# The down matrices of a mixture of experts loaded in two units of adjacent rows, with the middle rows turned at a stride

## The chip, the cores and the metric

The kernel runs on one core of a Trainium2 chip. The metric is the device time of one execution in microseconds (us); lower is better.

## What is computed

Two layers of a first block (three attention mixers side by side, a layer norm, a mixture of experts with a gated side path, a second norm), then two layers of a second block, all on 256 tokens of width 1024, in float32. The change touches the experts of the first block and little else. What counts there is this (16 experts, each 1024 x 512 for gate and up, 512 x 1024 for down; every token picks two experts):

```
scores = sigmoid(h @ router_w)            # choose 1 of 4 groups, then 2 of its 4 experts
gate = one_hot(idx) * wts                 # weights of the two chosen
out = 0
for e in range(16):
    hid = silu(h @ w_gate[e]) * (h @ w_up[e])
    out = out + gate[..., e:e + 1] * (hid @ w_down[e])
h = layer_norm(alpha * h + out + side_path)
```

## The kernel before

**Weights.** All weights are streamed from HBM in units of 1 MB, 128 partitions x 2048 values, in one fixed list (`weight_plan`; for the experts `add_experts`). SyncE issues one DMA per unit (L379) into one of up to six raw buffers as soon as VectorE has read the unit that was there before. ScalarE rounds the unit to a high part (`split_scalar`, L387, two halves of 1024), VectorE subtracts to get the low part (`split_vector`, L392, two halves), and TensorE multiplies with both. There are three split buffers, so ScalarE's split of a unit waits until TensorE has finished with the unit three places earlier. `Feed` makes both engines split two units ahead: when an engine's program reaches the use of unit u, it first splits unit u + 2.

**An expert.** Each expert e has six units: gate 0 and 1, up 0 and 1, and then down 0 and 1 of expert e - 1. At most 64 tokens go to an expert in the fast path; `pick` gathers the tokens of four experts at once. High and low parts of the 64 tokens lie side by side as 128 columns, so that one pass with the high and one with the low part of the weights is a whole product. TensorE does, in iteration e:

- gate product of e, 16 matmuls of 512 columns (`up`, L1448 and L1451)
- `add_to_tokens(e - 2, 1)`: four matmuls (L1494) that put the second 512 columns of the result of e - 2 back into the token rows (in PSUM banks 4 to 7)
- `turn_hidden(e - 1)`: 8 float32 matmuls (16 passes in the trace, L1473) that turn the gate and up rows, 128 columns each, so that the hidden values lie along the partitions
- up product of e, 16 matmuls; after every fourth expert also `pick` (L1434, L1442)
- down products of e - 1, for each half of the output columns 8 matmuls
- `add_to_tokens(e - 1, 0)`: four matmuls for the first 512 columns

The order is written out by hand in the same way for ScalarE and VectorE; every engine works through its own list in order and waits on semaphores. After the turn ScalarE takes silu (L1572), VectorE multiplies (L1709), ScalarE makes the high part (L602), VectorE the low part (L605). After a half of the down product ScalarE scales it and writes the high part (L1583), VectorE the low part (L1718) into the single tile pair `expert_rows_hi` / `expert_rows_lo`, 512 wide; so ScalarE's second write waits for the first half's adds ("add e 0"). GpSimd makes the matrix that puts rows back to tokens (L1750) after the last adds of the expert before.

**Layout of a down unit.** Unit `half` holds the 512 columns of that half of all 512 rows: partition p holds rows p, 128 + p, 256 + p and 384 + p, in four runs of 2 KB. The turned hidden rows stand in the same order.

**Other tiles.** `junk` (128 x 1024) takes the unread output of squares (L655, L675), the sigmoids of the side path, and some start tables. `arena` is one tile from which views are cut by `mem(start, n)`.

Of the kernel before, what the change touches and what calls it, by code (L numbers as in the profile page):

```python
# [8 lines left out]
I32 = mybir.dt.int32  # L9
# [245 lines left out]
def build(nc, a, out):  # L255
    with ExitStack() as ctx:
# [15 lines left out]
        junk = sb("junk", [P, D])  # L272
# [8 lines left out]
        y_e = (sb("expert_rows_hi", [P, 512], F32R), sb("expert_rows_lo", [P, 512], F32R))  # L281
# [339 lines left out]

        gained = mem(6144, NT * D).rearrange("p (t d) -> p t d", t=NT)
# [29 lines left out]
        def norm_squares(act, label, t):  # L652
            act.wait_ge(*sig.now("junk_act"))
            act.wait_ge(*sig.at("norm_dve", f"{label} mean{t}"))
            act.activation(junk[:, :], h[:, t, :], ACT.Square, bias=stat[t][:, 1:2],  # L655
# [16 lines left out]
        def squares(act, src, total, *label):  # L672

            act.wait_ge(*sig.now("junk_act"))
            act.activation(junk[:, 0:src.shape[1]], src, ACT.Square, accum_out=total).then_inc(*sig.mark("junk_act", *label))  # L675
# [36 lines left out]
        pos_i = junk[:, 0:2 * S].bitcast(I32).rearrange("p (a s) -> p a s", a=2)  # L712
        posk = junk[:, S:2 * S]
        lam_in = junk[:, 512:1024].rearrange("p (j l n) -> p j l n", l=DEPTH, j=4)
# [343 lines left out]
        def scalar_block1(act, feed, tables, l):  # L1058
# [81 lines left out]
            for t in range(NT):  # L1140
# [3 lines left out]
                for hd in range(4):  # L1144
                    squares(act, orow1[:, t, hd, :], so1[:, 4 * t + hd:4 * t + hd + 1], n_("diff squares"))
# [226 lines left out]
        sg_of = lambda i: junk[:, 512 * (i % 2):512 * (i % 2) + 512]  # L1372
# [3 lines left out]
        def tensor_experts(pe, l):  # L1376
# [111 lines left out]
            def add_to_tokens(e_, half):  # L1488
                if half == 0:
                    pe.wait_ge(*sig.at("moe_pool", n_(f"rows {e_}")))  # L1490
                pe.wait_ge(*sig.at("dve_took", n_(f"down {e_} {half}")))
                for t in range(NT):
                    for part in range(2):
                        last = pe.matmul(PS[:, 4 + 2 * t + half, :], from_slot[:, t * P:(t + 1) * P], y_e[part][:, :],  # L1494
                                         start=e_ == 0 and part == 0, stop=e_ == N_EXP - 1 and part == 1)
                    if t == 0 and half == 1 and e_ == N_EXP - 1:
                        last.then_inc(*sig.mark("ps", n_("ln2") + " t0"))
                last.then_inc(*sig.mark("ps", n_(f"add {e_} {half}")))
# [27 lines left out]
        def scalar_experts(act, feed, l):  # L1526
# [50 lines left out]
            def down(e_, half):  # L1577
                name = n_(f"down {e_} {half}")
                feed(name)
                act.wait_ge(*sig.at("ps", n_(f"add {e_} 0") if half else name))  # L1580
                if half == 0:
                    act.wait_ge(*sig.at("dve_took", n_(f"pick gate {e_ // GROUP}")))
                act.activation(y_e[0][:, :], PS[:, banks.of(name), :], ACT.Copy,  # L1583
                               scale=gate_of(e_ // GROUP)[:, e_ % GROUP:e_ % GROUP + 1]).then_inc(*sig.mark("moe_act", name))

            pick(0)
            for e_ in range(N_EXP + 1):
# [8 lines left out]
                if e_ > 0:  # L1596
                    down(e_ - 1, 0)
                    down(e_ - 1, 1)
# [64 lines left out]
        def vector_experts(dve, feed, l):  # L1663
# [50 lines left out]
            def down(e_, half):  # L1714
                name = n_(f"down {e_} {half}")
                feed(name)
# [824 lines left out]
```

## Time and profile before

| | us |
|---|---|
| median of 3 runs | 1946.6 |
| lowest, highest | 1943.07, 1947.17 |
| the profiled execution | 1943.74 |
| its span (first to last instruction) | 1942.5 |
| TensorE busy in it | 1801.3 (93%) |
| VectorE busy | 1362.5 (70%) |
| ScalarE busy | 1134.9 (58%) |
| GpSimd busy | 180.4 (9%) |

The rows below come from this one execution. Its own time stands 1.2 us above the span. Busy time of TensorE is modelled at its ends, so a busy engine need not be at its peak. Times in rows are microseconds from the start of the span; durations in the chain of waits are the time by which a piece moved the chain forward.

### The profile page before, as it was taken

What the parts mean: (1) busy time and instruction counts of PE and PEld (TensorE: products, weight loads), DVE (VectorE), ACT (ScalarE), POOL (GpSimd) and SP (SyncE); (2) the same over time, 40 slices, a digit from 0 to 9 for tenths busy, and PEclk for the clock granted to TensorE, in tenths of its full rate; (3) what the DMA queues carried; (4) which work ended last, traced back from release to release, by engine and by line L of the source; (5) the groups of instructions that cost most, each with busy time, mean ns of one, the idle gap of its engine ahead of it and who ended that gap; (6) DMA issues with size and microseconds to landing.
All of it is one profiled execution on the core that took longest, in us unless ns stands there. A gap on an engine that the chain in (4) does not pass through costs nothing.

```text
span 1942.5 us, 27994 instructions
## 1 busy us (share of the span) xinstructions
PE 1801.3 (93%) x11460; PEld 1565.2 (81%) x11460; DVE 1362.5 (70%) x1605; ACT 1134.9 (58%) x1574; POOL 180.4 (9%) x152
## 2 busy tenths in 40 slices
PE   6989998998799898989989999999999999999998
PEld 5867776776598687777768889988898989988987
DVE  6776999899737689989975675575556666566555
ACT  4565678788537468888864545444444644444443
POOL 1000412301000032321010000000000000000000
PEclk9889999999889999999989999999999999999999
DMA  8334599998552459999865545646555545555552
GB/s 250 111 114 173 223 346 346 339 331 331 185 150 88 140 200 382 326 334 358 324 239 170 159 131 174 197 150 217 174 195 171 179 131 159 181 181 184 193 188 87
DMA packets 209444, 413.19 MB, mean 213 GB/s; under 512 B 16384, under 2 KB 130816, under 8 KB 192928
## 3 DMA queue, kind: packets, MB, share of 16 engines
q1 hardware_dynamic: 208224, 409.76, 61.2%
q8 instruction: 95, 1.56, 0.3%
q10 hardware_dynamic: 1088, 1.57, 0.3%
q14 instruction: 37, 0.30, 0.0%
HBM read 409.47 MB, written 1.84 MB: 212 GB/s over the span
## 4 chain that ended last, share of the span: by engine, by line
PE 69%; DVE 22%; ACT 5%; issue 2%; DMA 1%; POOL 0%; SPq 0%; DVEq 0%; ACTq 0%
DVE weights_lo L392 14%; PE PS L407 10%; PE PS L411 10%; PE PS L408 10%; PE PS L415 7%; PE PS L418 6%; PE PS L419 6%; PE PS L1448 4%; PE PS L1451 4%; PE PS L1494 3%; PE PS L1473 3%; ACT weights_hi L387 2%; PE PS L1434 1%; DVE expert_rows_lo L1718 1%; PE PS L434 1%
## 5 line engine op out<-in xcount | busy, mean ns | idle before, releaser
L392 DVE TENSOR_TENSOR weights_lo<-weights_raw,weights_hi 128x1024 fp32r<-128x1024 f32 x564 | 661.0, 1218 | 210.0 <-ACT weights_hi L387 209.2
L387 ACT ACTIVATE weights_hi<-weights_raw 128x1024 fp32r<-128x1024 f32 x564 | 560.7, 1045 | 125.3 <-PE PS L419 76.3
L407 PE MATMUL PS<-hT_hi,weights_hi 128*128 128x256 f32 (+1 forms) x1488 | 427.4, 287 | 18.0 <-ACT weights_hi L387 11.5
L411 PE MATMUL PS<-hT_hi,weights_lo 128*128 128x256 f32 (+1 forms) x1488 | 424.5, 285 | 1.2 <-DVE weights_lo L392 1.2
L408 PE MATMUL PS<-hT_lo,weights_hi 128*128 128x256 f32 (+1 forms) x1488 | 424.4, 285 | 0.0
L407 PEld LDWEIGHTS PS<-hT_hi,weights_hi 128*128 128x128 f32 (+1 forms) x1488 | 285.1, 192 | 25.2 <-issue 19.7
L411 PEld LDWEIGHTS PS<-hT_hi,weights_lo 128*128 128x128 f32 (+1 forms) x1488 | 285.0, 192 | 2.4 <-DVE weights_lo L392 1.9
L408 PEld LDWEIGHTS PS<-hT_lo,weights_hi 128*128 128x128 f32 (+1 forms) x1488 | 285.2, 192 | 1.8
L392 DVE TENSOR_TENSOR weights_lo<-arena,weights_hi 128x1024 fp32r<-128x1024 f32 x128 | 150.9, 1220 | 16.4 <-ACT weights_hi L387 15.5
L415 PE MATMUL PS<-weights_hi,opa_hi 128*128 128x512 f32 x384 | 153.5, 400 | 3.0 <-DVE opa_lo L605 2.8
L418 PE MATMUL PS<-weights_lo,opa_hi 128*128 128x512 f32 x384 | 152.5, 397 | 0.0
L419 PE MATMUL PS<-weights_hi,opa_lo 128*128 128x512 f32 x384 | 152.2, 396 | 0.0
L387 ACT ACTIVATE weights_hi<-arena 128x1024 fp32r<-128x1024 f32 x128 | 128.1, 1051 | 0.0
L415 PE MATMUL PS<-weights_hi,hT_hi 128*128 128x256 f32 (+2 forms) x384 | 120.6, 314 | 2.1 <-DVE hT_lo L605 1.8
L670 POOL TENSOR_TENSOR small<-small,const 128x1 f32<-128x1 f32 (+2 forms) x26 | 20.9, 806 | 1085.3 <-DVE small L641 842.6
L418 PE MATMUL PS<-weights_lo,hT_hi 128*128 128x256 f32 (+2 forms) x384 | 119.0, 310 | 0.1
L419 PE MATMUL PS<-weights_hi,hT_lo 128*128 128x256 f32 (+2 forms) x384 | 118.9, 310 | 0.0
L1750 POOL TENSOR_SCALAR opb_lo<-arena,const 128x256 fp32r<-128x256 f32 x32 | 72.8, 2275 | 440.4 <-PE PS L1494 440.4
L1448 PE MATMUL PS<-weights_hi,hT_hi 128*128 128x512 f32 x256 | 103.7, 405 | 0.3
L1451 PE MATMUL PS<-weights_lo,hT_hi 128*128 128x512 f32 x256 | 101.4, 396 | 0.3 <-DVE weights_lo L392 0.3
L1451 PE MATMUL PS<-weights_lo,hT_lo 128*128 128x512 f32 x256 | 101.3, 396 | 0.4 <-DVE weights_lo L392 0.4
L1448 PE MATMUL PS<-weights_hi,hT_lo 128*128 128x512 f32 x256 | 101.2, 395 | 0.0
(322 smaller groups left out, 3192.1 us busy)
## 6 DMA issues: line engine op xcount, KB each, us to landing
weights_raw<-in_w_in SPq DMA_DIRECT2D x80, 1024.0 KB, 5.7
weights_raw<-in_w_ff SPq DMA_DIRECT2D x64, 1024.0 KB, 5.3
weights_raw<-in_w_up SPq DMA_DIRECT2D x34, 1024.0 KB, 7.2
weights_raw<-in_w_down SPq DMA_DIRECT2D x34, 1024.0 KB, 7.3
weights_raw<-in_w_gate SPq DMA_DIRECT2D x30, 1024.0 KB, 7.3
arena<-in_w_down SPq DMA_DIRECT2D x30, 1024.0 KB, 6.8
arena<-in_w_gate SPq DMA_DIRECT2D x18, 1024.0 KB, 7.0
params<-in_w_gate SPq DMA_DIRECT2D x16, 1024.0 KB, 6.6
```

Source lines behind the costliest of these rows:

```text
L387: act.activation(u.flat[0][:, c:e], u.x[:, c:e], ACT.Copy).then_inc(*sig.mark("w_hi", u.u, i))
L392: dve.tensor_tensor(u.flat[1][:, c:e], u.x[:, c:e], u.flat[0][:, c:e].bitcast(F32), ALU.subtract).then_inc(*sig.mark("w_lo", u.u, i))
L407: pe.matmul(o, w[0], x[0], start=start, stop=False)
L408: pe.matmul(o, w[0], x[1], start=False, stop=False)
L411: return pe.matmul(o, w[1], x[0], start=False, stop=stop)
L415: pe.matmul(o, x[0], w[0], start=start, stop=False)
L418: pe.matmul(o, x[0], w[1], start=False, stop=False)
L419: return pe.matmul(o, x[1], w[0], start=False, stop=stop)
L1448: pe.matmul(o, x, w[0], start=start, stop=False)
L1451: return pe.matmul(o, x, w[1], start=False, stop=stop)
L1473: last = pe.matmul(PS[:, b, (4 * j + c) * SLOTS:(4 * j + c + 1) * SLOTS], gate_up[e_ % 2][:, j, c * P:(c + 1) * P], fold, start=True, stop ...
L1750: pool.tensor_scalar(from_slot, slot_b[:, e_, :], col(COL_PART), None, ALU.is_equal).then_inc(*sig.mark("moe_pool", n_(f"rows {e_}")))
```

## The change

1. `add_experts`: a down matrix is cut by rows. Partition p holds rows 4p to 4p + 3; unit i holds rows 4p + 2i and 4p + 2i + 1, all 1024 columns, one run of 8 KB for a partition.
2. `turn_hidden`: to match, the columns of a block c are those with index 4f + c, taken at a stride of four values (16 bytes).
3. Down product: both units feed both output halves, each half in its own PSUM bank; for the last expert the first half is finished before the second is begun.
4. `expert_rows` has a place for each half. The adds of both halves of expert e - 2 stand together, after the gate product of e and after the turn of e - 1. ScalarE and VectorE split the next two units, and then take the two halves.
5. `junk` is gone; what was written there goes to parts of `arena`.

```diff
-        for half in range(2 if e > 0 else 0):
-            w = a["w_down"][l, e - 1][:, 512 * half:512 * half + 512]
-            plan.append((f"down {e - 1} {half} {l}", w.rearrange("(k p) n -> p k n", p=P), 4, 512))
+        for i in range(2 if e > 0 else 0):
+            w = a["w_down"][l, e - 1].rearrange("(p k) n -> p k n", p=P)
+            plan.append((f"down {e - 1} {i} {l}", w[:, 2 * i:2 * i + 2, :], 2, D))
...
-        junk = sb("junk", [P, D])
...
-        y_e = (sb("expert_rows_hi", [P, 512], F32R), sb("expert_rows_lo", [P, 512], F32R))
+        y_e = (sb("expert_rows_hi", [P, 2, 512], F32R), sb("expert_rows_lo", [P, 2, 512], F32R))
...
-        posf = mem(8192, 512).rearrange("p (a s) -> p a s", a=2)
+        posf = mem(4608, 512).rearrange("p (a s) -> p a s", a=2)
...
-        sg_of = lambda i: junk[:, 512 * (i % 2):512 * (i % 2) + 512]
+        sg_of = lambda i: mem(9216 + 512 * (i % 2), 512)
...
-                                         gate_up[e_ % 2][:, j, c * P:(c + 1) * P], fold, start=True, stop=True)
+                                         gate_up[e_ % 2][:, j, :].rearrange("p (f c) -> p c f", c=4)[:, c, :], fold, start=True,
+                                         stop=True)
...
-            def down(e_, half):
-                name = n_(f"down {e_} {half}")
-                u = use(pe, name)
-                b = banks.take(pe, name, "dve_took", among=4)
-                if half == 0:
-                    pe.wait_ge(*sig.at("moe_dve", n_(f"hidden {e_}")))
-                for k in range(4):
-                    last = two_pass(PS[:, b, :], hid_e[e_ % 2][:, k, :, :].rearrange("p c s -> p (c s)"), u,
-                                    at_k(u.pair, k, 0, 512), k == 0, k == 3, k == 0)
-                last.then_inc(*sig.mark("ps", name))
...
+            def down(e_):
+
+                us = [units[place[n_(f"down {e_} {i}")]] for i in range(2)]
+                b = [banks.take(pe, n_(f"down {e_} half {half}"), "dve_took", among=4) for half in range(2)]
+                parts = [(i, half) for i in range(2) for half in range(2)]
+                if e_ == N_EXP - 1:
+                    parts = [(i, half) for half in range(2) for i in range(2)]
+                pe.wait_ge(*sig.at("moe_dve", n_(f"hidden {e_}")))
+                for i, half in parts:
+                    fresh = half == 0
+                    if fresh:
+                        use(pe, us[i].name)
+                    for k in range(2):
+                        last = two_pass(PS[:, b[half], :], hid_e[e_ % 2][:, 2 * i + k, :, :].rearrange("p c s -> p (c s)"), us[i],
+                                        at_k(us[i].pair, k, 512 * half, 512 * half + 512), i == k == 0, i == k == 1,
+                                        fresh and k == 0)
+                    if half == 1:
+                        last.then_inc(*sig.mark("ps", us[i].name))
+                        if i == 1:
+                            sig.also("ps", n_(f"down {e_} half 1"))
+                    elif i == 1:
+                        last.then_inc(*sig.mark("ps", n_(f"down {e_} half 0")))
...
             for e_ in range(N_EXP + 1):
                 if e_ < N_EXP:
                     up(e_, "gate")
-                if e_ > 1:
-                    add_to_tokens(e_ - 2, 1)
                 if e_ > 0:
                     turn_hidden(e_ - 1)
+                if e_ > 1:
+                    add_to_tokens(e_ - 2)
                 if e_ < N_EXP:
                     up(e_, "up")
                     if e_ % GROUP == GROUP - 1 and e_ + 1 < N_EXP:
                         pick(e_ // GROUP + 1)
                 if e_ > 0:
-                    down(e_ - 1, 0)
-                    down(e_ - 1, 1)
-                    add_to_tokens(e_ - 1, 0)
-            add_to_tokens(N_EXP - 1, 1)
+                    down(e_ - 1)
+            add_to_tokens(N_EXP - 1)
...
-            def down(e_, half):
-                name = n_(f"down {e_} {half}")
-                feed(name)
-                act.wait_ge(*sig.at("ps", n_(f"add {e_} 0") if half else name))
-                if half == 0:
-                    act.wait_ge(*sig.at("dve_took", n_(f"pick gate {e_ // GROUP}")))
-                act.activation(y_e[0][:, :], PS[:, banks.of(name), :], ACT.Copy,
-                               scale=gate_of(e_ // GROUP)[:, e_ % GROUP:e_ % GROUP + 1]).then_inc(*sig.mark("moe_act", name))
+            def down(e_):
+                feed(n_(f"down {e_} 0"), n_(f"down {e_} 1"))
+                act.wait_ge(*sig.at("dve_took", n_(f"pick gate {e_ // GROUP}")))
+                for half in range(2):
+                    name = n_(f"down {e_} half {half}")
+                    act.wait_ge(*sig.at("ps", name))
+                    if e_ > 0:
+                        act.wait_ge(*sig.at("ps", n_(f"add {e_ - 1} {half}")))
+                    act.activation(y_e[0][:, half, :], PS[:, banks.of(name), :], ACT.Copy,
+                                   scale=gate_of(e_ // GROUP)[:, e_ % GROUP:e_ % GROUP + 1]).then_inc(*sig.mark("moe_act", name))
...
```

VectorE's `down` changes in the same way as ScalarE's (feed both units, then both halves), and `add_to_tokens` now loops over both halves and waits, before each, for VectorE's low part of that half.

## Rows read from the trace of the kernel before

**Rows 1.** The page's chain that ended last, by engine and by line.
```profile
PE 69%; DVE 22%; ACT 5%; issue 2%; DMA 1%; POOL 0%; SPq 0%; DVEq 0%; ACTq 0%
DVE weights_lo L392 14%; PE PS L407 10%; PE PS L411 10%; PE PS L408 10%; PE PS L415 7%; PE PS L418 6%; PE PS L419 6%; PE PS L1448 4%; PE PS L1451 4%; PE PS L1494 3%; PE PS L1473 3%; ACT weights_hi L387 2%; PE PS L1434 1%; DVE expert_rows_lo L1718 1%; PE PS L434 1%
```
**Rows 2.** Stretches, two experts: length, busy PE, PEld, DVE, ACT, POOL; clock, DMA, GB/s.
```profile
307.20:324.76 17.56, 15.58 (x74) 12.06 (x74) 15.95 (x17) 14.38 (x19) 2.29 (x1) 1.00 0.96 344
324.76:342.34 17.58, 15.61 (x74) 12.06 (x74) 16.00 (x17) 14.43 (x19) 2.32 (x1) 1.00 0.98 351
```
**Rows 3.** Chain of waits through one expert: start us, us, piece.
```profile
324.76 1.75 PE PS L1473 x16
...
328.81 6.90 DVE weights_lo L392 x6
335.71 0.67 DVE expert_rows_lo L1718
...
336.51 1.16 PE PS L1494 x4
337.68 0.24 PE PS L1448
...
341.41 0.92 PE PS L1494 x4
```
**Rows 4.** VectorE's timeline in two experts: start, us, instruction [idle before <- releaser].
```profile
326.94 0.42 DVE L1709 TENSOR_TENSOR arena<-arena,PS 128x256 f32<-128x256 f32 x1 [0.48 <-ACT arena L1572]
...
327.85 0.42 DVE L605 TENSOR_TENSOR opb_lo<-arena,opb_lo 128x256 fp32r<-128x256 f32 x1 [0.48 <-ACT opb_lo L602]
...
328.81 2.36 DVE L392 TENSOR_TENSOR weights_lo<-arena,weights_hi 128x1024 fp32r<-128x1024 f32 x2 [0.53 <-ACT weights_hi L387]
...
357.23 0.75 DVE L1718 SCALAR_TENSOR_TENSOR expert_rows_lo<-PS,small,expert_rows_hi 128x512 fp32r<-128x512 f32 x1 [0.35 <-ACT expert_rows_hi L1583]
...
358.18 2.36 DVE L392 TENSOR_TENSOR weights_lo<-arena,weights_hi 128x1024 fp32r<-128x1024 f32 x2 [0.20 <-ACT weights_hi L387]
```
**Rows 5.** L1709 from 232.1 to 492.9: idle before it, us and times.
```profile
  ACT arena L1572: 6.1, 13
```
**Rows 6.** L1473, the weight loads of all turns: ns min/median/max.
```profile
L1473 PEld LDWEIGHTS PS<-const,arena x512: 187/192/333, 231.9 to 1007.1; 128*128 128x128 f32 x171
```
**Rows 7.** L602 and L605: reads of h (strided) and of dense tiles, ns min/median/max.
```profile
L602 ACT ACTIVATE opa_hi<-h x4: 2319/2327/2332, 190.9 to 691.2; 128x1024 fp32r<-128x1024 f32 x4
L602 ACT ACTIVATE hT_hi<-arena x2: 1040/1048/1056, 6.4 to 7.3; 128x1024 fp32r<-128x1024 f32 x2
...
L605 DVE TENSOR_TENSOR opa_lo<-h,opa_hi x4: 2140/2182/2228, 198.2 to 698.5; 128x1024 fp32r<-128x1024 f32 x4
L605 DVE TENSOR_TENSOR hT_lo<-arena,hT_hi x2: 1219/1222/1226, 7.5 to 8.6; 128x1024 fp32r<-128x1024 f32 x2
```
**Rows 8.** SyncE's waits (us, times, longest); issues and landings of two units.
```profile
SPq L379 <- DVE weights_lo L392: 1555.5, 355, 21.0
...
313.63 0.38 SPq L379 DMA_DIRECT2D arena<-in_w_down  x1
...
318.17 0.34 SPq L379 DMA_DIRECT2D weights_raw<-in_w_gate  x1
...
arena<-in_w_down SPq DMA_DIRECT2D x1, 1024.0 KB, 7.8
...
weights_raw<-in_w_gate SPq DMA_DIRECT2D x1, 1024.0 KB, 8.4
```
**Rows 9.** Tail of layer 0: timeline, then one stretch as in rows 2.
```profile
499.65 2.35 DVE L392 TENSOR_TENSOR weights_lo<-arena,weights_hi 128x1024 fp32r<-128x1024 f32 x2
...
505.65 0.50 PE L1494 MATMUL PS<-expert_rows_hi,opb_lo 128*128 128x512 f32 x1 [1.66 <-DVE expert_rows_lo L1718]
...
510.50 0.77 PE L1448 MATMUL PS<-weights_hi,opb_lo 128*128 128x512 f32 x1 [1.93 <-DVE opb_lo L605]
...
519.61 1.22 DVE L628 SCALAR_TENSOR_TENSOR h<-h,PS 128x1024 f32<-128x1024 f32 x1 [0.82 <-PE PS L1494]
...
511.00:514.50 3.50, 3.50 (x11) 2.71 (x10) 2.24 (x2) 1.20 (x2) 0.00 (x0) 0.62 0.04 8
```

More of the change, by code:

```diff
@@ L620, in turned_lo @@
                 lo_part(dve, hT[1][sl], one_bank(banks.of(name), 4), hT[0][sl]).then_inc(*sig.mark("dve_took", name))
+        unread, unread2 = mem(8192, D), mem(6144, 512)
         gained = mem(6144, NT * D).rearrange("p (t d) -> p t d", t=NT)
@@ L670, in rstd, with squares @@
             return pool.tensor_tensor(dst, var, col(COL_NHALF).to_broadcast([P, var.shape[1]]), ALU.pow)
-        def squares(act, src, total, *label):
+        def squares(act, src, total, *label, dst=None):
             act.wait_ge(*sig.now("junk_act"))
-            act.activation(junk[:, 0:src.shape[1]], src, ACT.Square, accum_out=total).then_inc(*sig.mark("junk_act", *label))
+            act.activation((unread if dst is None else dst)[:, 0:src.shape[1]], src, ACT.Square, accum_out=total).then_inc(
+                *sig.mark("junk_act", *label))
         def softmax_vector(dve, label, t, scale, st, fix, chain):
@@ L1144, in scalar_block1 @@
                 for hd in range(4):
-                    squares(act, orow1[:, t, hd, :], so1[:, 4 * t + hd:4 * t + hd + 1], n_("diff squares"))
+                    squares(act, orow1[:, t, hd, :], so1[:, 4 * t + hd:4 * t + hd + 1], n_("diff squares"),
+                            dst=mem(9216, 512))
             feed(n_("w_o 1"))
@@ L1488, in add_to_tokens @@
-            def add_to_tokens(e_, half):
-                if half == 0:
[L1490 to L1498, printed above, removed]
+            def down(e_):
[19 more added lines that the diff above has]
+                        last.then_inc(*sig.mark("ps", n_(f"down {e_} half 0")))
@@ new lines, in add_to_tokens @@
+            def add_to_tokens(e_):
+                for half in range(2):
+                    if half == 0:
+                        pe.wait_ge(*sig.at("moe_pool", n_(f"rows {e_}")))
+                    pe.wait_ge(*sig.at("dve_took", n_(f"down {e_} half {half}")))
+                    for t in range(NT):
+                        for part in range(2):
+                            last = pe.matmul(PS[:, 4 + 2 * t + half, :], from_slot[:, t * P:(t + 1) * P], y_e[part][:, half, :],
+                                             start=e_ == 0 and part == 0, stop=e_ == N_EXP - 1 and part == 1)
+                        if t == 0 and half == 1 and e_ == N_EXP - 1:
+                            last.then_inc(*sig.mark("ps", n_("ln2") + " t0"))
+                    last.then_inc(*sig.mark("ps", n_(f"add {e_} {half}")))
@@ L1575, in turn_hidden @@
                     *sig.mark("moe_act", name))
-            def down(e_, half):
-                name = n_(f"down {e_} {half}")
-                feed(name)
-                act.wait_ge(*sig.at("ps", n_(f"add {e_} 0") if half else name))
-                if half == 0:
-                    act.wait_ge(*sig.at("dve_took", n_(f"pick gate {e_ // GROUP}")))
-                act.activation(y_e[0][:, :], PS[:, banks.of(name), :], ACT.Copy,
-                               scale=gate_of(e_ // GROUP)[:, e_ % GROUP:e_ % GROUP + 1]).then_inc(*sig.mark("moe_act", name))
+            def down(e_):
+                feed(n_(f"down {e_} 0"), n_(f"down {e_} 1"))
+                act.wait_ge(*sig.at("dve_took", n_(f"pick gate {e_ // GROUP}")))
+                for half in range(2):
+                    name = n_(f"down {e_} half {half}")
[4 more added lines that the diff above has]
+                                   scale=gate_of(e_ // GROUP)[:, e_ % GROUP:e_ % GROUP + 1]).then_inc(*sig.mark("moe_act", name))
             pick(0)
@@ L1596, in scalar_experts @@
                 if e_ > 0:
-                    down(e_ - 1, 0)
-                    down(e_ - 1, 1)
+                    down(e_ - 1)
             act.wait_ge(*sig.at("route_dve", n_("flag")))
@@ L1712, in turn_hidden, with down @@
                         hid_e[e_ % 2][:, :, 0, :]).then_inc(*sig.mark("moe_dve", n_(f"hidden {e_}")))
-            def down(e_, half):
-                name = n_(f"down {e_} {half}")
-                feed(name)
-                dve.wait_ge(*sig.at("moe_act", name))
-                dve.scalar_tensor_tensor(y_e[1][:, :], PS[:, banks.of(name), :],
-                                         gate_of(e_ // GROUP)[:, e_ % GROUP:e_ % GROUP + 1], y_e[0][:, :].bitcast(F32),
-                                         ALU.mult, ALU.subtract).then_inc(*sig.mark("dve_took", name))
+            def down(e_):
+                feed(n_(f"down {e_} 0"), n_(f"down {e_} 1"))
+                for half in range(2):
+                    name = n_(f"down {e_} half {half}")
+                    dve.wait_ge(*sig.at("moe_act", name))
+                    dve.scalar_tensor_tensor(y_e[1][:, half, :], PS[:, banks.of(name), :],
+                                             gate_of(e_ // GROUP)[:, e_ % GROUP:e_ % GROUP + 1], y_e[0][:, half, :].bitcast(F32),
+                                             ALU.mult, ALU.subtract).then_inc(*sig.mark("dve_took", name))
             pick(0)
@@ L1732, in vector_experts @@
                 if e_ > 0:
-                    down(e_ - 1, 0)
-                    down(e_ - 1, 1)
+                    down(e_ - 1)
         def gpsimd_experts(pool, l):
@@ L2066, in gla_rows @@
                 for hd in range(4):
-                    squares(act, orow2[:, t, hd, :], so2[:, 4 * t + hd:4 * t + hd + 1], n_("gla squares"))
+                    squares(act, orow2[:, t, hd, :], so2[:, 4 * t + hd:4 * t + hd + 1], n_("gla squares"), dst=unread2)
             feed(n_("gmlp v0"))
@@ L2076, in scalar_block2 @@
                 act.wait_ge(*sig.at("gmlp_dve", n_(f"centred {t}")))
-                squares(act, vz[:, t, :], sz[t][:, 2:3], n_(f"gmlp squares {t}"))
+                squares(act, vz[:, t, :], sz[t][:, 2:3], n_(f"gmlp squares {t}"), dst=unread2)
             for i, name in enumerate(L("mix q0", "mix q1")):
```

8 lines of the change are left out of this document (4 added, 4 removed).

## The prediction

> **What bounds the kernel now.** I read the page's chain of waits first: TensorE holds 69% of it, VectorE 22%, and the costliest single line is L392, VectorE making the low halves of the weights [rows 1]. Both shares are means over stages, and the change touches two stages only, the experts of layer 0 (about 232 to 519 us) and of layer 1 (about 730 to 1020 us). So I read one expert there. The busy times of two neighbouring experts show 17.57 us each, with VectorE busy for 16.0, TensorE for 15.6 (a modelled figure), ScalarE for 14.4 and the DMA engines for 96 to 98% [rows 2]. None is full, so a chain through several engines must close the cycle.
>
> The chain shows it [rows 3]: the turn on TensorE (1.75 us, 16 passes), ScalarE and VectorE taking it, six low halves on VectorE without a gap (6.90), the first row block of the down product (0.67), then four matmuls adding these rows to the tokens (1.16), 16 gate matmuls (337.68 to 341.41, 3.73 us, 0.233 each), four more adds (0.93), and the next turn. TensorE waits for VectorE at the first adds, and VectorE then waits for TensorE behind the turn. VectorE's own idle time per expert is small: 0.48 us before L1709, waiting for the silu after the turn; 0.48 before L605; 0.53 before the first low half of the down matrix; in the experts with a pick another 0.35 + 0.20 before L1718 and L392 [rows 4]. The first kind sums to 6.1 us in 13 waits from 232 to 493 us [rows 5]; one more follows at the last expert, and the first one of a layer, with no adds before its turn, will stay. Check of the cycle by VectorE: 12 halves at 1.15 (6.90 / 6) = 13.8, two row blocks at 0.67, two takings at 0.44, idle 0.48 + 0.48 + 0.53: 17.5.
>
> **The change, part by part.**
> 1. *Adds moved behind the turn.* Both halves' adds (8 matmuls, 8 x 0.233 = 1.9 us) now come after the next gate product and after the turn. The path from the down product to the next turn loses 1.16 + 0.93 us. ScalarE no longer waits for "add e 0" before the second row block, since the row blocks have two places. The turn then ends well ahead: from the last down low half (time 0), gate low halves are ready at 2.3 and 4.6, row blocks end at 6.0, the two up units at 8.3 and 10.6; TensorE ends gate at 4.6 + 1.7 = 6.3, turns until 8.05, and the silu (0.39) is there at 8.5, some 2 us before VectorE asks at 10.6. So the 0.48 wait goes, 13 times a layer: 6.1 us. What is late next is VectorE itself: 13.8 + 1.34 + 0.88 + 1.01 = 17.05 us per expert. The idle 0.48 and 0.53 stay, for they lie between VectorE and ScalarE (product, high part, low part, split).
> 2. *Does other work still fit?* TensorE: gate, up and down 48 matmuls, 8 adds: 56 x 0.233 = 13.05, and 1.75 for the turn, 14.8 of 17.05. ScalarE 14.4. The split of down unit 1 waits for up unit 0: turn 8.05, adds to 9.9, up unit 0 to 11.8; ScalarE comes to it at 13.4. GpSimd's rows for the next expert (2.3 us) start after the adds and have over 12 us. Taking both down banks at once waits for the gate's bank and the last row block, both long free. Nothing is queued in front of anything that VectorE needs soon.
> 3. *Pick experts (three a layer).* Both gate units are now split before the row blocks. ScalarE's second split still waits for the first down unit, so 0.37 of the 0.55 us [rows 4] stays: 0.2 x 3 = 0.5 us.
> 4. *Tail of a layer.* Before: the last turn waits for adds that wait for VectorE's second row block; TensorE idles 1.66 us, then 1.93 us, and starts the last down product at 510.50; the sum into h starts at 519.61 [rows 9]. After, from the same start of the low halves (499.65): halves to 504.3, row blocks to 505.6, with the turn and silu already done by 503.9; the hidden low part ends near 507.0, adds end at 507.1, twelve of the sixteen down matmuls at 509.9. Here one step costs: ScalarE is fed both next units before the row blocks, and its second split waits until these twelve are done, 1.9 us more, so the rows come at 512.5 and 513.1, VectorE's at 513.9 and 514.6 and the sum starts near 515.6. That is 4.0 us earlier. If TensorE is at its 1.2 GHz level in this product, as it mostly is now (granted clock 0.62 of full speed from 511 to 514.5, after the two idle stretches, [rows 9]), about 1.5 less.
> 5. *The strided turn.* Each of the 16 loads of a turn reads 128 columns with 16 bytes between them, where it read them side by side. No load in this trace has a stride. Its own row says 0.109 us a load (1.75 / 16, [rows 3]; 16 records an expert over 32 experts are the 512 of [rows 6]), the floor. The ceiling comes from other engines: ScalarE and VectorE read h with 32 bytes between elements at 2327 and 2182 ns for 1024 elements, against 1048 and 1222 side by side [rows 7]. That is about 1.25 and 0.94 ns an element more, roughly 2 ns an element: 128 x 2.05 = 262 ns a load, 4.2 us a turn, 2.45 us more. I take the floor, for it is the same engine and instruction, and keep both ends. Up to about 3.4 us a turn costs nearly nothing: TensorE has 17.05 - 14.8 = 2.25 us left, less some 0.6 for starts after waits.
> 6. *Transfers.* A down unit goes from 512 runs of 2 KB to 128 runs of 8 KB. The queue waits for VectorE to free a buffer, not the reverse; the waits of SyncE's queue at L379 name VectorE 355 times [rows 8]. So this is worth 0 now. Cadence rises from 6.29 MB per 17.57 us (358 GB/s) to per 17.05 (369). Two units issued at 313.63 and 318.17, one more between them, landed 7.8 and 8.4 us later [rows 8], at 321.4 and 326.6: 2.57 us a unit, 15.4 an expert, so it fits. Of 17 us between uses of a buffer, landing takes 7.8 to 8.4.
> 7. *Junk tile gone* (squares, sigmoids, start tables written into the arena): same instructions, same waits; 0, bounded by a few hundred ns at the start.
>
> The Trainium skill ("SBUF — State Buffer", section "Door 1: The DMA port swizzle") says that memory lines are 16 bytes and that reads that take only one element of each line pay. [Rows 7] agree with it at 32 bytes for two engines; for a TensorE load no row shows it. By the rule the turn slows; by its own row it doesn't.
>
> **Sum.** Per layer 6.1 + 0.5 + 4.0 = 10.6, less about half of the tail's clock doubt (0.7): 9.9; two layers 19.8. Profiled run 1943.7 (span 1942.5 and 1.2 around it): 1923.9. The median of the runs shown is 1946.6, 2.9 above the profiled one, so the same gain would make 1926.8. I predict 1926.
>
> **Rivals.**
> - *The turn's loads slow down past the slack* (slower than before). One mechanism, at L1473: each load at 2 ns a column. For it: [rows 7] and TensorE's chain through the turn. Against: other engines, a wider stride. It decides from 3.4 us a turn; each us above is paid by 15 experts. At 4.2: 0.8 x 15 + 1.4 for the pick experts = 13.4 per layer, against 9.9 gained: 7 us slower, 1951 (1954 on the median's scale). Break-even is near 4.0. At 5 us a turn it would be 1975.
> - *Partly slow* (3.5 to 3.9 us a turn): 1932 to 1943.
> - *Transfers are the limit.* The DMA engines are 96 to 98% busy already [rows 2]. Were 358 GB/s the most that comes, an expert stays at 17.57 and only parts 3 and 4 are left, 2 x 4 = 8 us: 1937. Against: the 2.57 us a unit, and landings at 7.8 to 8.4 that don't grow without end.
>
> The Trainium skill ("DMA: Bandwidth & Descriptors", "Specifications") gives about 358 GB/s of memory bandwidth per core, which is today's cadence to the digit; by it this last rival would be the outcome. The 2.57 us a unit (408 GB/s) speaks against it here.
>
> **How the numbers follow.** Forecast, with the turn under 3.4 us: 0.60, 1920 to 1932 (tail clock, scale of the runs). Partly slow turn: 0.08. Transfers: 0.07. Slow turn: 0.22, 1946 to 1975. No change for some reason not seen: 0.03. About 0.2% (4 us) is what a measurement tells from no change. Faster by over that: 0.60 + 0.05 of the partly slow + 0.06 of the transfers = 0.71; within: 0.03 of the partly slow, 0.01 of the transfers, 0.02 of the slow turn and 0.03 unseen = 0.09; slower: 0.20. The range 1918 to 1955 leaves out the slow turn's far end and little else.
>
> **What would show it.** Right: the wait of L1709 for L1572 gone but for the first expert, VectorE idle only at L605 and the first down half, 17.05 us per expert, the 16 passes of a turn within 3.4 us, adds without waits for L1718, the sum into h 4 us sooner after the last low halves. Wrong if: the span of a turn's 16 passes is above 3.4 us and TensorE has no idle time left; or splits (L387) wait for landings; or the silu still comes late. In the stages outside the experts nothing should move by more than 1 us.

## The result, and the profile after

| | before | after |
|---|---|---|
| median | 1946.6 us (5 runs, 1943.07 to 1949.29) | 1955.72 us (5 runs, 1955.2 to 1959.39) |
| span of the profiled execution | 1942.5 | 1955.9 |

The change made the kernel slower: ratio 1.0053, 95% interval 1.0037 to 1.0069, 9.1 us between the medians. The forecast was 1926. The two profiled executions, of which all readings below are, lie further apart, 13.4 us. Nearly all of that lies in the two expert stages. From the first matmul on `slot_T` (the start of the gathering of tokens on TensorE) to the sum into h, layer 0 takes 317.3 us instead of 310.0 and layer 1 takes 317.7 instead of 311.7, 13.3 in all; the stretches ahead of, between and behind them moved by 0.1 to 0.2 us each.

The chain of the whole kernel, first the shares by engine, then by line:

```profile
PE 75%; DVE 18%; ACT 4%; issue 1%; DMA 1%; POOL 0%; SPq 0%; ACTq 0%; DVEq 0%
DVE weights_lo L391 11%; PE PS L406 10%; PE PS L410 10%; PE PS L407 10%; PE PS L414 7%; PE PS L417 6%; PE PS L418 6%; PE PS L1476 6%; PE PS L1453 5%; PE PS L1450 4%; PE PS L1511 4%; ACT weights_hi L386 2%; PE PS L1436 2%; PE PS L433 1%; DMA weights_raw<-in_w_in 1%
```

Against [rows 1], TensorE has gone from 69 to 75% and VectorE from 22 to 18%. The turn (now L1476) has doubled its share from 3 to 6%, while the low halves (now L391) went from 14 to 11%. The group of the turn's loads, with busy time and mean ns, says why; in [rows 6] the same loads had a median of 192 ns:

```profile
L1476 PEld LDWEIGHTS PS<-const,arena 128*128 128x128 f32 x512 | 122.0, 327 | 1.5
```

In the chain one sees the length of a turn directly:

```profile
308.09 3.56 PE PS L1476 x16
311.66 2.98 PE PS L1511 x8
314.64 0.43 PE PS L1450
315.06 0.43 PE PS L1453
...
327.14 3.55 PE PS L1476 x16
330.69 1.90 PE PS L1511 x8
332.60 0.23 PE PS L1450
...
334.56 1.07 ACT weights_hi L386
335.63 0.02 issue
335.65 2.36 DVE weights_lo L391 x2
338.03 4.64 DVE weights_lo L391 x4
342.68 0.04 issue
342.72 0.50 PE PS L1453
```

A turn takes 3.56 us where [rows 3] had 1.75: 0.222 us for each of 16 loads, 2.03 times as long. The second thing to see stands right behind it. The eight adds (L1511) take 1.90 us behind one turn and 2.98 behind the other, and the first matmuls after those are at 0.43 instead of 0.23. Windows over the same four pieces (length, busy times, then granted clock, DMA share, GB/s) show it in the clock:

```profile
308.09:311.66 3.57, 3.57 (x18) 3.57 (x17) 3.57 (x4) 1.60 (x3) 0.00 (x0) 1.00 1.00 353
311.66:314.64 2.98, 2.98 (x9) 2.33 (x9) 1.86 (x4) 2.46 (x4) 0.00 (x0) 0.58 1.02 366
327.14:330.69 3.55, 3.55 (x17) 3.55 (x17) 3.55 (x4) 1.66 (x3) 0.00 (x0) 1.00 0.97 339
330.69:334.60 3.91, 3.91 (x19) 3.15 (x18) 2.81 (x5) 2.75 (x5) 0.92 (x1) 1.00 0.99 367
```

TensorE shows as busy the whole time. In the turn its granted clock is 1.00 (2.4 GHz); from 311.66 the mean is 0.58, so it stood at the 1.2 GHz level for most of that stretch. Behind 11 of 30 turns with adds the eight adds take 2.9 to 3.3 us in this way. The expert of the first piece (308.09 to 327.14) is 19.05 us long, the next one 17.49, so a fall costs about 1.55.

The last thing is what closes the cycle now. VectorE's timeline in this expert (start, us, instruction, idle before it and releaser), with ScalarE's one line that it hangs on:

```profile
331.15 0.42 DVE L1725 TENSOR_TENSOR arena<-arena,PS 128x256 f32<-128x256 f32 x1
332.05 0.43 DVE L604 TENSOR_TENSOR opb_lo<-arena,opb_lo 128x256 fp32r<-128x256 f32 x1 [0.48 <-ACT opb_lo L601]
333.00 2.37 DVE L391 TENSOR_TENSOR weights_lo<-arena,weights_hi 128x1024 fp32r<-128x1024 f32 x2 [0.53 <-ACT weights_hi L386]
335.65 4.74 DVE L391 TENSOR_TENSOR weights_lo<-weights_raw,weights_hi 128x1024 fp32r<-128x1024 f32 x4 [0.28 <-ACT weights_hi L386]
```

```profile
334.56 2.01 ACT L386 ACTIVATE weights_hi<-weights_raw 128x1024 fp32r<-128x1024 f32 x2 [0.63 <-PE PS L1453]
```

The wait of [rows 5] before the product is gone: L1725 has no bracket. The other two, 0.48 and 0.53, are those of [rows 4]. New is 0.28 us at 335.65: ScalarE's split of down unit 1 waits for the buffer that up unit 0 had, and TensorE reaches that product late, behind turn and adds. The chain goes through TensorE there, so a longer turn is felt as soon as this split waits.

### The profile page after: what moved, and what is told of

It is laid out like the page before. It is cut to its first block, busy times and chain, and to the rows that moved or that the text cites. A ratio compares the mean times of both kernels' runs of the same rounds, so it can differ in the third digit from the quotient of the medians.

```text
span 1955.9 us, 28024 instructions
## 1 busy us (share of the span) xinstructions
PE 1867.7 (95%) x11460; PEld 1638.8 (84%) x11460; DVE 1364.8 (70%) x1605; ACT 1135.6 (58%) x1574; POOL 156.8 (8%) x152
## 4 chain that ended last, share of the span: by engine, by line
PE 75%; DVE 18%; ACT 4%; issue 1%; DMA 1%; POOL 0%; SPq 0%; ACTq 0%; DVEq 0%
DVE weights_lo L391 11%; PE PS L406 10%; PE PS L410 10%; PE PS L407 10%; PE PS L414 7%; PE PS L417 6%; PE PS L418 6%; PE PS L1476 6%; PE PS L1453 5%; PE PS L1450 4%; PE PS L1511 4%; ACT weights_hi L386 2%; PE PS L1436 2%; PE PS L433 1%; DMA weights_raw<-in_w_in 1%
## 5 line engine op out<-in xcount | busy, mean ns | idle before, releaser
L391 DVE TENSOR_TENSOR weights_lo<-weights_raw,weights_hi 128x1024 fp32r<-128x1024 f32 x564 | 663.2, 1219 | 235.4 <-ACT weights_hi L386 234.4
L391 DVE TENSOR_TENSOR weights_lo<-arena,weights_hi 128x1024 fp32r<-128x1024 f32 x128 | 151.2, 1221 | 17.1 <-ACT weights_hi L386 17.1
L1476 PEld LDWEIGHTS PS<-const,arena 128*128 128x128 f32 x512 | 122.0, 327 | 1.5
L1476 PE MATMUL PS<-const,arena 128*128 128x64 f32 x512 | 119.2, 386 | 0.0
```

The costliest lines, as they stand in the source:

```text
L391: dve.tensor_tensor(u.flat[1][:, c:e], u.x[:, c:e], u.flat[0][:, c:e].bitcast(F32), ALU.subtract).then_inc(*sig.mark("w_lo", u.u, i))
```

## The experiments

Ten kernels, all but one timed in five rounds beside the kernel before, in three groups (the first four, the next four, the last two). Kernels of different groups are compared by their ratios to the kernel before, whose median was 1945.7, 1943.7 and 1946.3 us in the three groups. Theory S ("the stride") in short: the strided load is slow, the long turn costs some time, and the falls of the clock cost the rest; without the stride the change does what the forecast said.

**Dense.** The change, but a unit takes rows p, 128 + p, ... in runs of 4 KB, and the turn reads side by side.

```diff
-  w = a["w_down"][l, e - 1].rearrange("(p k) n -> p k n", p=P)
+  w = a["w_down"][l, e - 1].rearrange("(k p) n -> p k n", p=P)
-  gate_up[e_ % 2][:, j, :].rearrange("p (f c) -> p c f", c=4)[:, c, :]
+  gate_up[e_ % 2][:, j, c * P:(c + 1) * P]
```

> Edit: changed kernel, but a down unit holds two adjacent blocks of 128 rows (runs of 4 KB), so the turn reads its columns side by side again; all else as in the changed kernel. Theory S (the stride: slow loads of the turn close the loop on TensorE, and the clock falls behind them): turn back at 1.75 us, no fall of the granted clock after a turn, 17.05 us per expert, VectorE idle only before L604 and the first down half; 1922 to 1930 us. Rival O (the new order of adds, turn and down product costs by itself, the stride is hidden): stays at 1950 or more.

Measured: 1918.84 us, ratio 0.9862 [0.9848, 0.9877], 3 us below the range; the turn's loads 191 ns, and no fall behind the 28 turns that come before the last one of a layer. Its chain through one expert is VectorE's, with ScalarE in one gap:

```profile
299.82 1.32 DVE expert_rows_lo L1735 x2
301.14 4.54 DVE weights_lo L391 x4
305.68 0.34 DVE arena L1725
...
306.37 1.06 ACT weights_hi L386
307.43 0.02 issue
307.45 9.17 DVE weights_lo L391 x8
316.62 1.32 DVE expert_rows_lo L1735 x2
```

16.8 us an expert. The stride costs 36.9 us (1955.72 - 1918.84), and everything else in the change together gains 27.

**Stride of 8 bytes.** Unit i takes rows 256 i + 2p and 2p + 1, again one run of 8 KB; a turn's load takes every second value.

```diff
-  w[:, 2 * i:2 * i + 2, :]                     # of "(p k) n -> p k n"
+  w[256 * i:256 * i + 256, :].rearrange("(p k) n -> p k n", p=P)
-  .rearrange("p (f c) -> p c f", c=4)[:, c, :]
+  .rearrange("p (h f c) -> p h c f", h=2, c=2)[:, c // 2, c % 2, :]
```

> Edit: unit i of a down matrix holds rows 256 i + 2p and 256 i + 2p + 1 (one run of 8 KB for a partition, as in the changed kernel), so the turn takes every second column, 8 bytes apart. Theory S with lines of 16 bytes (two loaded values share one): loads as fast as dense ones, turn 1.75 us, the time of the dense kernel within 2 us. Rival: any stride slows a load, turn 2.3 us or more. Since runs of 8 KB are kept, a difference to the dense kernel in landing times would show what the longer runs are worth; I expect none in the total.

Measured: 1920.91 us, ratio 0.9870 [0.9853, 0.9887]; loads 196 ns. Every second value (two in each 16 bytes) costs nothing that counts, and 8 KB runs gain nothing over 4 KB.

**The kernel before with the stride alone.** Only the turn's columns and the order of the rows of the down matrix are changed, with the old halves and 2 KB runs.

```diff
-  gate_up[e_ % 2][:, j, c * P:(c + 1) * P]
+  gate_up[e_ % 2][:, j, :].rearrange("p (f c) -> p c f", c=4)[:, c, :]
-  w.rearrange("(k p) n -> p k n", p=P)
+  w.rearrange("(p k) n -> p k n", p=P)
```

> Edit: the kernel before, with a down half-unit holding rows 4p to 4p + 3 (runs of 2 KB as before) and the turn at a stride of 16 bytes; order untouched. Theory S: the turn is on the closed path there, so each of 30 experts pays the whole 1.8 us: 54 us, and more where the clock falls: 1995 to 2020 us. Rival O: no effect of the stride, 1944 to 1950.

Measured: 2006.35 us, ratio 1.0314 [1.03, 1.0328].

```profile
314.98 3.57 PE PS L1473 x16
...
318.57 0.39 ACT arena L1572
...
318.98 0.43 DVE arena L1709
...
320.84 6.90 DVE weights_lo L392 x6
327.74 0.67 DVE expert_rows_lo L1718
```

The loop of [rows 3] is unchanged and 1.82 us longer, from one turn to the next 19.4 us. In this kernel the turn is on the path with its whole length: 32 x 1.8 = 58 of the 60 us. So the change's new order hides part of the turn, and without it the stride would have cost more.

**Dense, every turn matmul issued twice.** This is the length of the turn without the stride.

```diff
-  for j in range(2):
-      for c in range(4):
+  for j, c in [(j, c) for j in range(2) for c in range(4) for _ in range(2)]:
```

> Edit: the dense kernel of this set with each matmul of the turn issued twice (32 passes with dense loads, about 3.5 us, the length of the strided turn, with twice the columns streamed in that time). If a turn of 3.5 us alone made the time, it costs what the changed kernel costs, 1956. If the clock falls because the slow loads feed the array thinly, the clock stays up here, experts take 17.4 to 17.5 us, and the time is 1936 to 1942 (the changed kernel less its 11 falls at about 1.5 us).

Measured: 1937.54 us, ratio 0.9962 [0.995, 0.9974].

```profile
324.15 3.52 PE PS L1475 x32
327.67 1.90 PE PS L1510 x8
```

The turn is as long as in the change, 17.4 us an expert, and in no case do the eight adds behind it take over 1.97 us. So the length costs 18.7 us over the dense kernel, and some 18 us more (ratio 0.9962 against 1.0053) separate this kernel from the change: 11 falls of 1.55 are 17.

**Dense, adds ahead of the turn.** Is the adds' new place worth anything?

```diff
-                if e_ > 0:
-                    turn_hidden(e_ - 1)
                 if e_ > 1:
                     add_to_tokens(e_ - 2)
+                if e_ > 0:
+                    turn_hidden(e_ - 1)
```

> The dense variant (turn loads side by side, down units of 4 KB runs), with both halves' adds put back in front of the turn, everything else kept. By my theory the two places of the row block and the early splits already took the adds off VectorE's path: from the last down low half, row blocks end at 6.0 us, gate at 6.3, adds at 8.2, turn at 9.9, silu at 10.4, and VectorE asks for it at 10.6. So nothing or a few tenths an expert: 1919 to 1924 us, against 1918.8 with the adds behind the turn. The rival, that the gain of the dense variant comes from the adds' place behind the turn: the 0.48 us wait for the silu returns at 13 experts a layer or more, 1930 or above.

Measured: 1937.36 us, ratio 0.9963 [0.9949, 0.9977]. By the ratios the new place is worth 1.0%, 20 us, where I had expected at most 5: I had counted the steady expert alone. It is 17.0 us there instead of 16.8, and over the 14 intervals between the first and the fifteenth product of a layer that makes 3.2 us. The larger part is the last expert of a layer. VectorE's timeline there:

```profile
500.56 1.40 DVE L1735 SCALAR_TENSOR_TENSOR expert_rows_lo<-PS,small,expert_rows_hi 128x512 fp32r<-128x512 f32 x2
507.30 0.42 DVE L1725 TENSOR_TENSOR arena<-arena,PS 128x256 f32<-128x256 f32 x1 [5.34 <-ACT arena L1587]
```

With no gate product left to hide them, the adds wait for both row blocks, the turn for the adds, and VectorE idles 5.34 us. The part of the layer from the fifteenth product to the sum into h takes 30.5 us, against 26.6 and 25.6 in the dense kernel. The two expert stages together are 15.6 us longer in the trace; the other 3 us between the two profiled spans (1937.6 and 1919.0) stand ahead of the first expert stage, where the edit changes nothing, and are no effect of it. The time fits the rival's range (1930 or above), but its mechanism doesn't: from the second to the fifteenth product VectorE waits for the silu by 0.1 to 0.2 us an expert, not by 0.48.

**Dense, one next unit behind the row blocks.** At the last expert of a layer, ScalarE and VectorE split the second of the next two units after the row blocks.

```diff
-                feed(n_(f"down {e_} 0"), n_(f"down {e_} 1"))
+                late = e_ == N_EXP - 1
+                feed(n_(f"down {e_} 0"), *(() if late else (n_(f"down {e_} 1"),)))
...
+                if late:
+                    feed(n_(f"down {e_} 1"))
```

> The dense variant, but the last expert of a layer splits only one of the next units ahead of its row blocks and the other behind them. My theory of the tail: ScalarE's second split there waits for twelve down matmuls and holds the first row block back; with it moved, the sum into h starts 1.9 us earlier in each layer or more (in the dense variant's chain, split 1.07 and two low halves 2.36 us stand between the twelfth down matmul and the row block): 1912 to 1917 us against 1918.8. Rival: the matmuls at the low granted clock or the late landing of the last down unit set that end, and the split moved behind only delays the next stage's weights: 1918 to 1921.

Measured: 1915.75 us, ratio 0.9855 [0.984, 0.987]. The same part of the layer now takes 22.3 and 23.2 us, 4.3 and 2.4 less. The row blocks come first, and the split that stood in front of them follows:

```profile
501.72 0.75 DVE L1739 SCALAR_TENSOR_TENSOR expert_rows_lo<-PS,small,expert_rows_hi 128x512 fp32r<-128x512 f32 x1
503.53 0.75 DVE L1739 SCALAR_TENSOR_TENSOR expert_rows_lo<-PS,small,expert_rows_hi 128x512 fp32r<-128x512 f32 x1 [1.06 <-ACT expert_rows_hi L1601]
504.48 2.36 DVE L391 TENSOR_TENSOR weights_lo<-weights_raw,weights_hi 128x1024 fp32r<-128x1024 f32 x2 [0.19 <-ACT weights_hi L386]
506.76 1.21 DVE L628 SCALAR_TENSOR_TENSOR h<-h,PS 128x1024 f32<-128x1024 f32 x1
```

The span is 1913.6 us against 1919.0. The ratio moved only from 0.9862 to 0.9855, and the intervals overlap, so the earlier sum into h is shown in the traces, but a gain in the times is not.

**The change's rows, permuted by ScalarE.** 8 KB runs and rows 4p to 4p + 3 as in the change; ScalarE's copy of the gate and up products puts value 4f + c at place 128c + f, and the turn reads side by side. So ScalarE reads in order and writes with 512 bytes from one value to the next; the 16 bytes of the expectation are the distance in the product of values that become neighbours, not that of the writes.

```diff
-  act.activation(gate_up[e_ % 2][:, j, :], PS[:, b, :], ACT.Copy)
+  act.activation(gate_up[e_ % 2][:, j, :].rearrange("p (c f) -> p f c", c=4),
+                 PS[:, b, :].rearrange("p (f c) -> p f c", c=4), ACT.Copy)
```

> The change's own 8 KB runs with rows 4p to 4p+3 to a partition, but the permutation is paid by ScalarE: it writes the gate and up products with 16 bytes between neighbours, so that the turn's loads read side by side again. If only the stride of TensorE's load costs, the whole loss goes: turn 1.75 us, loads near 190 ns, no fall of the granted clock behind the turn, 1918 to 1925 us. If ScalarE's writes pay for the stride as its reads do (584 ns becoming 1.2 us twice an expert), ScalarE has 1.3 us more of about 16.8 and stays under VectorE: 1919 to 1926. Rival, the layout in memory (which rows of the down matrix a partition gets, or 8 KB runs) costs something itself: above 1935.

Measured: 1923.44 us, ratio 0.9901 [0.9884, 0.9919].

```profile
L1579 ACT ACTIVATE arena<-PS 128x512 f32<-128x512 f32 x64 | 70.5, 1101 | 0.0
L1476 PEld LDWEIGHTS PS<-const,arena 128*128 128x128 f32 x512 | 62.1, 191 | 2.9
```

ScalarE pays too, 1101 ns instead of 585 for a copy, and comes into the chain of every expert (16.97 us each instead of 16.80). With the layout in memory kept and the stride moved off TensorE's load, 1.5% (30 us) of the 1.9% (37 us) come back.

**Stride of 32 bytes.** The changed kernel with the turn's columns 8 values apart; it turns other columns than it should, so the hidden values differ, at the same amount of work.

```diff
-  gate_up[e_ % 2][:, j, :].rearrange("p (f c) -> p c f", c=4)[:, c, :]
+  gate_up[e_ % 2].rearrange("p j n -> p (j n)").rearrange("p (f c) -> p c f", c=8)[:, 4 * j + c, :]
```

> The changed kernel, but each turn load reads its 128 columns 32 bytes apart instead of 16 (it takes other columns of the hidden rows than it should, so the hidden values are wrong; the amount of work is the same). Theory: a load pays when it takes only one value of each 16 bytes, and no more for a wider distance: loads again 0.222 us each, turn 3.56 us, 1950 to 1962 us. Rival: the cost grows with the distance, as 8 bytes free and 16 bytes double may be two points of a slope: turn 5 to 7 us, 1985 us or more.

Measured, in a single run: 1962.54 us, turn 3.63 us.

```profile
L1476 PEld LDWEIGHTS PS<-const,arena 128*128 128x128 f32 x512 | 124.4, 333 | 1.5
```

Hardly more than at 16 bytes (327 ns). The cost is no slope: next to none at 8 bytes (196), the turn doubled at 16, the same at 32. The run is just above the 1950 to 1962 of theory S, and its trace has more falls of the clock behind turns than the change, 14 instead of 11.

**The stride with wider matmuls.** The last question is what takes the clock down. In the changed kernel, seven of the eight turn matmuls stream 128 columns instead of 64 behind the same strided load. Half of each of these results is junk, which the next matmul overwrites; for that the eight are issued in reverse order.

```diff
-                for j in range(2):
-                    for c in range(4):
+                for j in (1, 0):
+                    for c in (3, 2, 1, 0):
+                        n = SLOTS if j == c == 0 else 2 * SLOTS
-                        last = pe.matmul(PS[:, b, (4 * j + c) * SLOTS:(4 * j + c + 1) * SLOTS], ..., fold,
+                        last = pe.matmul(PS[:, b, (4 * j + c + 1) * SLOTS - n:(4 * j + c + 1) * SLOTS], ...,
+                                         const[:, C_FOLD + SLOTS - n:C_FOLD + SLOTS],
```

> The changed kernel with its 16-byte stride, but each of a turn's matmuls streams 128 columns instead of 64 behind the same load (the upper half of each result is overwritten by the next one), so that TensorE multiplies for more of the 0.222 us that a load takes. The dense kernel with every turn issued twice lasted as long in the turn (3.52 us) and kept its granted clock; the changed kernel lost it in 11 of 31 experts. Theory: the clock falls because TensorE multiplies little while it waits for the slow loads; with more columns behind each load the falls get rarer or go, the turn stays at 3.5 to 3.8 us, and the time is 1936 to 1944 us (11 falls of 1.55 us less). Rival: the slow loads alone, or the turn's length together with the waits around it, bring the falls: 1952 to 1959 us, falls as often as before.

Measured: 1937.45 us, ratio 0.9958 [0.9941, 0.9974]. The turn is as long (3.55 us), its loads as slow (328 ns), and no fall is left behind any of the 30 turns, where the changed kernel has 11 (the expectation's 31 is a miscount). Two turns with the adds behind them, by windows:

```profile
322.16:325.71 3.55, 3.55 (x17) 3.55 (x17) 3.55 (x4) 1.65 (x3) 0.00 (x0) 1.00 0.98 351
325.71:327.60 1.89, 1.89 (x9) 1.56 (x9) 1.20 (x3) 1.36 (x3) 0.00 (x0) 1.00 0.91 355
```

By the ratios, 0.9958 against 1.0053, useless work made the kernel 18 us faster. Length of the turn and loads are those of the change; what differs is how much TensorE multiplies meanwhile. So the falls come neither from the length nor from the slow load as such. The dense kernel with every turn matmul issued twice (1937.54 us) agrees: the same length, no falls, the same time.

**Both good parts.** Stride of 8 bytes with the late split.

> 8 KB runs as in the change, but a unit takes rows 256 i + 2p and 2p + 1, so that the turn's loads stand 8 bytes apart, and the last expert of a layer splits the second next unit behind its row blocks. Both parts have been measured apart: 1920.9 for the 8-byte stride, 1915.8 for the tail in the dense variant against 1918.8 without. If they add, 1916 to 1919 us, equal to the dense variant with the tail within 2 us. Rival: 8 KB runs move transfers enough to show once the tail is shorter: outside 1913 to 1920.

Measured: 1915.93 us, ratio 0.9845 [0.9827, 0.9862], within its interval the same as the dense kernel with the late split. Of everything that ran, these two are the fastest: 30 us under the kernel before and 40 under the change.

## Why the prediction was wrong

The product of the hidden rows (VectorE, L1725) marks an expert. From the traces, per layer, in us: (a) 14 intervals from the first product to the fifteenth, (b) from the fifteenth to the sum into h; layer 0 / layer 1.

| kernel | turn | (a) | (b) |
|---|---|---|---|
| before | 1.75 | 258.3 / 258.1 | 26.4 / 28.3 |
| after | 3.56 | 265.6 / 263.6 | 24.8 / 27.4 |
| dense | 1.75 | 248.8 / 248.8 | 26.6 / 25.6 |
| dense, turn twice | 3.52 | 257.0 / 257.0 | 24.8 / 24.8 |
| dense, adds first | 1.75 | 252.0 / 252.0 | 30.5 / 30.5 |
| dense, late split | 1.75 | 248.9 / 248.9 | 22.3 / 23.2 |
| wide turn | 3.55 | 257.5 / 257.6 | 23.9 / 23.5 |

**Part 5 is the step that failed,** in three places. First the size: I took the floor of 0.109 us a load "for it is the same engine and instruction", and it was 0.222, nearer to the ceiling of 0.262 that came from other engines' rows. [Rows 7] were the better witness: a value read at a distance cost ScalarE 1.25 and VectorE 0.94 ns more, and now TensorE's load 0.88 (0.113 us over 128 columns). The Trainium skill ("SBUF — State Buffer", "Door 1: The DMA port swizzle") has the rule: lines of 16 bytes, of which at least two reads in a row must fall into the same one for full speed. The three measured distances agree with it: two values in a line are as good as free, one is not, and 32 bytes are hardly worse than 16.

Second, "up to about 3.4 us a turn costs nearly nothing". A turn of 3.52 us without any stride costs 0.62 us an expert and 18.7 in all. My account of TensorE's free time was a sum, 2.25 of 17.05 us; it asked how much TensorE does in an expert, not when. The turn starts only behind seven matmuls of the gate product that wait for VectorE's last gate half (from 342.72 on in the chain above; the next turn starts at 344.63), and the split of down unit 1 hangs on the up product behind the turn and the adds. I had worked out this very wait in part 2, with ScalarE coming to it 1.6 us behind TensorE (13.4 against 11.8). A turn that is 1.8 us longer uses that up, but I never walked through the schedule again with the longer turn. By my own price a turn of 3.56 us would have cost 0.16 x 15 = 2.4 us a layer, 5 in all; its length alone cost nearly four times that, 18.7.

Third, what no part had and the sum put at nothing: the falls of the clock. In part 4 I read [rows 9] as the cost of idle stretches; I didn't ask what else a slow load could do to it, with TensorE shown as busy all the time. 11 falls of 1.55 are 17 us, and the wide turn gives 18 back. With them gone the change would be faster than the kernel before (1937.45), inside what I called partly slow. The rival "slow turn" named the right place and sign; its break-even near 4.0 was wrong, for the change already lost at 3.56.

**Part 1, adds behind the turn: right, and too small.** The silu waits went (13 x 0.48 to next to nothing), and the dense kernel runs at 16.80 us an expert, not 17.05. The halves are 13.71 us, not 13.8, and takings with idle time 1.76, not 1.89: instructions that follow each other overlap by some 0.08 us, and I had added whole durations. Over 14 intervals a layer gains 9.4 us, where I had 6.1 + 0.5.

**Part 2, other work fits: right for 1.75 us** (in the dense kernel splits wait for TensorE only in the experts with a pick and at the end of a layer), wrong for the turn that came.

**Part 3, the pick experts: wrong in sign, and small.** I gave them 0.2 us on top of the common gain. Ordinary experts went from 17.56 to 16.80 us, those with a pick only from 21.61 to 21.27, so they gain 0.4 less, not 0.2 more. ScalarE's second split does wait for the first down unit, as I said, but by 1.15 us, for the pick on TensorE stands ahead of it (the first line below, from the dense kernel).

```profile
279.46 2.01 ACT L386 ACTIVATE weights_hi<-arena 128x1024 fp32r<-128x1024 f32 x2 [1.15 <-PE PS L1453]
...
488.70 2.01 ACT L386 ACTIVATE weights_hi<-arena 128x1024 fp32r<-128x1024 f32 x2 [0.93 <-DMA arena<-in_w_down]
```

**Part 4, the tail: right in kind, too large in size.** Layer 0 gains 1.5 us in (b), layer 1 0.8, where I had 4.0. The 1.9 us that I named for the second split is there, and larger: the split (1.07) and VectorE's two low halves behind it (2.36) stand before the row blocks. The adds that end a layer run at the lower clock in both layers (2.9 us for six), those after the last turn in layer 1. The dense kernel gains nothing in layer 0 and 2.7 us in layer 1; in both its adds after the last turn run at the lower clock (0.58 from 495.74 to 499.14), and in layer 0 the last two down units land late besides (0.93 us of ScalarE's waiting, the second line above, and 0.77 for the next unit). Taking the split out gives 4.1 and 5.1 against the kernel before. That is no hit of the forecast: its 4.0 had the 1.9 us of the split in it, so without the split it would have said 5.9.

**Part 6, transfers: right.** Runs of 2, 4 or 8 KB make no difference, and the dense kernel takes 6.29 MB in 16.8 us, 374 GB/s, so that rival is dead. The Trainium skill ("DMA: Bandwidth & Descriptors", "Specifications") gives about 358 GB/s per core. That is not the limit here, where 374 were taken over whole experts. In the dense kernel units land late only at the end of layer 0, as just shown.

**Part 7: right,** the other stages moved by 0.2 us or less.

Open: what decides which of the 30 turns is followed by a fall. The 11 have the same length and the same loads as the other 19, their places have no order that I can read, and they differ between the layers (five in layer 0, six in layer 1).

## What to carry to other kernels

Before an operand is read at a stride, count how many of its values lie in each 16 bytes. With fp32, one value in each 16 bytes doubled the time of a TensorE load in the chain, where two were free (ScalarE's write of one value in each 512 bytes took 1.9 times as long); a layout in pairs of rows kept the long runs and lost nothing. When an operation may get longer, don't compare sums of busy time: walk through the schedule again with the longer piece, for the first wait behind it is what closes. And a TensorE that is shown as busy but multiplies little lost its clock in 11 of 30 cases here, so a slow load had a second price, which wider matmuls behind the same loads took away.

## What the hardware showed unexpectedly

- A 128 x 128 fp32 load of TensorE: 191 ns side by side, 196 with 8 bytes from value to value, 327 with 16, 333 with 32 (means of 512 records each).
- Behind turns of 16 slow loads and 64-column matmuls (3.56 us, TensorE busy all the time) the granted clock fell in 11 of 30 cases; with 128 columns, or with twice as many dense ones in the same time, in none of 30.
- The kernel before with the stride alone loses the clock behind turns too, but no time goes with it: what follows its turn is the up product, which isn't on the path there. Windows of one turn there and of the 4 us behind it:

```profile
353.79:357.36 3.57, 3.57 (x17) 3.57 (x17) 1.70 (x2) 0.36 (x1) 2.31 (x1) 1.00 1.02 402
357.36:361.36 4.00, 4.00 (x12) 3.09 (x12) 2.56 (x4) 3.33 (x5) 0.00 (x0) 0.57 0.94 379
```

The clock is 0.57, and its experts still take 19.4 us like those without a fall. In the change the adds and the up product behind the turn stand on the path, so the same fall costs 1.55 us.
